# Two 64-byte gaps between the high and low halves of a three-product float32 matmul

## The reference

```
proj = jnp.einsum('bsd,de->bse', h, w_in)                    # 2048 -> 15424
q    = jnp.einsum('bsr,re->bse', _rmsnorm(q_a, ...), w_q_b)  # 512 -> 3072
kv   = jnp.einsum('bsr,re->bse', _rmsnorm(c_kv, ...), w_kv_b)# 512 -> 4096
y_mla, y_conv = ... @ w_o_mla, ... @ w_o_conv                # 2048 -> 2048 each
out  = jnp.einsum('bsd,de->bse', merged, w_out)              # 2048 -> 2048
proj = h @ w_in_2                                            # second block, 272 rows with 16 meta tokens
p    = jnp.einsum('btnc,ncd->btnd', y, w_branch)             # 2 x (1024 -> 2048)
out  = ... @ w_out_2                                         # 2048 -> 2048
```

## Time and profile before

| | |
|---|---|
| median of three runs | 1954.52 us (1952.75 to 1959.03) |
| the profiled execution | 1953.02 us |
| its span, first to last instruction | 1951.6 us |
| PE (matmul) busy | 1937.9 us, 99% of the span, 15818 matmuls |
| PEld (weight load) busy | 1904.6 us, 98% |
| DVE busy | 1175.2 us, 60% |
| ACT busy | 880.6 us, 45% |
| POOL busy | 311.4 us, 16% |
| DMA | 343.80 MB, mean 176 GB/s |

### The profile page before, as it was taken

The page is one execution under the profiler, slowest core; times in us unless marked ns, Lnnn a source line. Parts: engine busy times, 40 slices in busy tenths (PEclk is TensorE's granted clock), DMA queues, the critical chain, the costliest instruction groups (busy, mean ns, idle before and its releaser), DMA issues.

```text
span 1951.6 us, 37152 instructions
## 1 busy us (share of the span) xinstructions
PE 1937.9 (99%) x15818; PEld 1904.6 (98%) x15818; DVE 1175.2 (60%) x1708; ACT 880.6 (45%) x1265; POOL 311.4 (16%) x317
## 2 busy tenths in 40 slices
PE   8999999999999999999999999999999999999999
PEld 8999999999999999999999999999999999999987
DVE  7765666556554545655564665676467776554644
ACT  6444454544444334544445543446443333444443
POOL 3210010202010001300122252040011232110200
PEclk9999999999999999999999999999999999999999
DMA  7565555566666556666565564444565444666564
GB/s 262 154 193 172 165 150 151 172 176 183 193 183 187 188 189 184 181 190 197 189 227 195 176 222 131 141 134 127 160 181 146 131 141 141 174 197 192 184 230 158
DMA packets 175920, 343.80 MB, mean 176 GB/s; under 512 B 10494, under 2 KB 19578, under 8 KB 175226
## 3 DMA queue, kind: packets, MB, share of 16 engines
q1 hardware_dynamic: 174106, 337.16, 56.9%
q10 hardware_dynamic: 1648, 4.26, 0.6%
HBM read 335.09 MB, written 6.29 MB: 175 GB/s over the span
## 4 chain that ended last, share of the span: by engine, by line
PE 94%; DVE 1%; issue 0%; POOL 0%; ACT 0%; POOLq 0%; ACTq 0%; DVEq 0%
PE bank L1289 93%; DVE w_lo L1932 0%; DVE hb L2168 0%; POOL scratch L2528 0%; PE bank L1506 0%; ACT w_hi L1624 0%; PE bank L1444 0%; PE bank L1595 0%; PE bank L1446 0%; PE bank L1445 0%; PE bank L1596 0%; DVE scratch L2038 0%; PE bank L1508 0%; POOL acc_a L2457 0%; POOL arena L2568 0%
## 5 line engine op out<-in xcount | busy, mean ns | idle before, releaser
L1932 DVE TENSOR_TENSOR w_lo<-w_raw,w_hi 128x1024 fp32r<-128x1024 f32 (+2 forms) x644 | 786.5, 1225 | 488.1 <-ACT w_hi L1624 486.7
L1624 ACT ACTIVATE w_hi<-w_raw 128x1024 fp32r<-128x1024 f32 (+2 forms) x644 | 662.9, 1032 | 899.0 <-PE bank L1289 890.0
L1289 PE MATMUL bank<-hb,w_hi 128*128 128x256 f32 x4896 | 868.1, 280 | 1.1 <-DVE hb L1956 0.9
L1289 PEld LDWEIGHTS bank<-hb,w_hi 128*128 128x128 f32 x4896 | 747.5, 188 | 4.1 <-DVE w_lo L1932 2.4
L1289 PE MATMUL bank<-hb,w_lo 128*128 128x256 f32 x2448 | 682.5, 279 | 0.0
L1289 PE MATMUL bank<-ob_hi,w_hi 128*128 128x256 f32 (+1 forms) x2224 | 641.3, 288 | 0.1
L1289 PE MATMUL bank<-ob_hi,w_lo 128*128 128x256 f32 (+1 forms) x2224 | 625.4, 281 | 0.0
L1289 PE MATMUL bank<-ob_lo,w_hi 128*128 128x256 f32 (+1 forms) x2224 | 625.0, 281 | 0.0
L1289 PEld LDWEIGHTS bank<-hb,w_lo 128*128 128x128 f32 x2448 | 460.0, 188 | 0.0
L1289 PEld LDWEIGHTS bank<-ob_hi,w_hi 128*128 128x128 f32 x2224 | 418.3, 188 | 2.5 <-DVE w_lo L1932 0.5
L1289 PEld LDWEIGHTS bank<-ob_lo,w_hi 128*128 128x128 f32 x2224 | 418.4, 188 | 1.6
(11 more groups left out here) (241 smaller groups left out, 1169.5 us busy)
## 6 DMA issues: line engine op xcount, KB each, us to landing
w_raw<-in_w_in SPq DMA_DIRECT2D x436, 512.0 KB, 3.7
w_raw<-in_w_out SPq DMA_DIRECT2D x64, 512.0 KB, 4.2
w_raw<-in_w_o_conv SPq DMA_DIRECT2D x32, 512.0 KB, 3.9
w_raw<-in_w_o_mla SPq DMA_DIRECT2D x32, 512.0 KB, 4.1
w_raw<-in_w_branch SPq DMA_DIRECT2D x32, 512.0 KB, 3.7
w_raw<-in_w_kv_b SPq DMA_DIRECT2D x16, 512.0 KB, 3.8
w_raw<-in_w_q_b SPq DMA_DIRECT2D x16, 384.0 KB, 3.3
arena<-x_kept SPq DMA_DIRECT2D x2, 2048.0 KB, 9.4
```

The costliest lines, as they stand in the source:

```text
L1289: return nc.tensor.matmul(dst, lhsT, rhs, start=start, stop=stop, skip_group_check=True)
L1624: act(dst, src, ACT.Copy).then_inc(S_("w_hi"), 1)
L1932: tt(low, src, high.bitcast(F32), ALU.subtract).then_inc(S_("w_lo"), 1)
```

## The change

Two dummy tensors of 16 floats (64 bytes) are put in, one between `w_hi` and `w_lo`, one between `ob_hi` and `ob_lo`; in `hb` the 64 bytes that lay ahead of both halves now lie between them, and the 64 bytes behind them are gone. All instructions, their order, their waits and their shapes stay as they were; only addresses differ.

```diff
         self.whi = sb("w_hi", [P, N_SPLIT, UNIT], F32R)
+        sb("apart", [P, ODD])
         self.wlo = sb("w_lo", [P, N_SPLIT, UNIT], F32R)
-        hb = sb("hb", [P, ODD + 2 * KT * S + ODD], F32R)[:, ODD:ODD + 2 * KT * S].rearrange("p (k n) -> p k n", k=2 * KT)
-        self.hb_hi, self.hb_lo = hb[:, 0:KT, :], hb[:, KT:2 * KT, :]
-        self.ob_hi, self.ob_lo = (sb(n, [P, KT, T + ODD], F32R)[:, :, 0:T] for n in ("ob_hi", "ob_lo"))
+        hb = sb("hb", [P, KT * S + ODD + KT * S], F32R)
+        self.hb_hi, self.hb_lo = (hb[:, at:at + KT * S].rearrange("p (k n) -> p k n", k=KT) for at in (0, KT * S + ODD))
+        self.ob_hi = sb("ob_hi", [P, KT, T + ODD], F32R)[:, :, 0:T]
+        sb("apart2", [P, ODD])
+        self.ob_lo = sb("ob_lo", [P, KT, T + ODD], F32R)[:, :, 0:T]
```

## The result

The changed kernel takes 1963.46 us (median of seven runs, 1962.88 to 1965.67) against 1956.16 us for the kernel before (seven runs, 1952.75 to 1960.95). The ratio is 1.0043 with a 95% interval from 1.0031 to 1.0055: slower by 0.43%, a small loss, but one that the interval sets apart from no change. The forecast was 1954 us and no change, with 1948 to 1960 us as its own range and 1922 to 1978 us with the rivals.

The account below looks back on a forecast made before the run. PE's distance from one matmul's start to the next was taken as the bound. All terms were 0: span 1951.6 + 0, profiled execution 1953.0, so 1954 us, no change; own range 1948 to 1960 us, 1922 to 1978 us with rivals.

Parts of the forecast that it names:

- the bound: PE, busy 99% of the span: an address change can act only on the distance between matmul starts.
- the cost of the moved tensors to DVE: Subtraction into w_lo, 1224 ns per unit: even a tenth more would go into DVE's idle time; put at 0.
- the two paces: In hb, 256 columns: 117.7 and 113.2 ns on the same addresses, a lock of PE's two streams that a break can switch.
- The sign named for "right": 565 to 640 us again holds 637 to 640 matmuls with 279 to 280 ns records; 1377 to 1396 us again 153.
- each pair of streams that run together keeps its distance exactly: 256-column products: moving operand and the weights loaded beside it keep their address distance modulo 8; 0 us.
- the broken alternation within a kind: 256-column products: the middle matmul starts on the other parity, breaking the alternation twice per triple; taken as 0, range -48 to +29 us.
- rival A: The parity break ends the slow pace: 1927 us for hb alone, 1906 us with ob too; chance 0.24.
- Rival C: Paces redrawn among stretches, 6 us either way, 1948 to 1960 us; beyond the bound 0.06 fast, 0.08 slow.
- Rival B: Equal parities of moving operand and weights clash in two of three pairs: 24 us slower, 1978 us; chance 0.24.
- its aside that the 272-column phases would get a little faster: 272-column stretch: a little faster if equal parities clash, since the same pairing now differs; no size given.
- The rule of the Trainium skill: TensorE has independent read ports for moving operand and weights, and PE never waits on anyone: the change gives 0.
- the 109.2 ns: The skill's back-to-back distance for a 256-column matmul, 256 / 2.4 + 2.5; no stretch of the trace reached it.

Follow-up runs that it names:

- the bare streams: Separate programs with none of the kernel's work: PE alone runs matmul triples at chosen operand placements behind short idle times; 256 columns paced from 113.3 to 120.0 ns.
- 3,4 with 2,3: The change's hb placement: starts of x_hi, x_lo with w_hi, w_lo in 64-byte units modulo 8; run alone on PE, 117.8 ns after all four idle times.
- 5,6 with 2,3: Placement with x_hi, x_lo starting at 5,6 and w_hi, w_lo at 2,3 (64-byte units modulo 8), run alone on PE: 118.5 ns in four of four.
- experiment 7: Kernel before with its tensors reordered and one gap, so hb's x minus w starts are 3 modulo 4 units: 1932.48 us, ratio 0.9878.
- the second trace of before: The kernel before, unchanged, traced once more: 1958.29 us, hb mean 117.42 ns instead of 116.80.
- the halves: Against the kernel before, only w_lo moved by 64 bytes: 1962.97 us; only x_lo, with arena and what lies behind it: 1967.32 us.
- experiment 4: Kernel before with only arena, con, scratch and all behind them moved by 64 bytes, products' operands in place: 1961.38 us, ratio 1.0018.
- 5,5 with 2,2: Placement with x_hi, x_lo both starting at 5 and w_hi, w_lo at 2 (64-byte units modulo 8), alone on PE: 113.3 ns, in some segments 117.8.

## Why the prediction was wrong

Right were the bound (PE's start-to-start distance and nothing else), that no other engine nor DMA sets the pace, that the cost of the moved tensors to DVE is nil (the subtraction into w_lo takes 1225 ns by either page), and that the steps to look at are the products. Right was also that the two paces are states of the same program: the bare streams show both on one placement without any other engine. The sign named for "right", 637 to 640 matmuls in 565 to 640 us, came out too (639), but it couldn't tell anything: that stretch was slow before the change already.

The step that failed is "each pair of streams that run together keeps its distance exactly. Cost: 0 us, if the pace hangs on that pair". The condition doesn't hold. With all distances kept, 3,4 with 2,3 and 5,6 with 2,3 were never fast in 16 segments each, hb in the changed kernel paces at 117.76 ns without a fast stretch, and the version of experiment 7 went from 1932.48 to 1968.88 us when the gaps were put in. Distance matters (6 of 51 against 40 of 52), but only among placements in which all x start at one parity and all w at one. I had seen the other side, the broken alternation within a kind, and given it a price from -48 to +29 us, but no mechanism of its own except as a gain (rival A). It was the reverse: with the break, no placement tried was ever fast (0 of 56 segments).

Rival C had the right place and nearly the right size, and the wrong kind. It said that both fast stretches would be drawn anew and priced their loss at 6 us; hb's mean rose by 0.96 ns, 7226 x 0.96 = 6.9 us (the 6 us had left out the fast matmuls of cin0, nearly 200). But it isn't an even draw: by the bare streams the fast pace is gone, so the loss comes in every run. Against the second trace of before, which had drawn badly, hb lost only 0.34 ns, or 2.5 us. The median of before's seven times, 1956.16 us, lies between the times of the two traces (1953.02 and 1958.29), so the typical loss in hb should lie between as well. To this come 3.0 us in ob, for which I had no term: with alternating blocks the placement of before paces at 117.06 to 117.10 and the changed one at 117.81.

Rival B read the higher pace of 272 columns as the price of equal parity. The bare streams give 126.6 to 126.7 ns at even and uneven starts alike, so its rows didn't bear on it. Its sign was right, and so was its aside that the 272-column phases would get a little faster, but its mechanism was false: the halves would have had to be faster than the whole.

The rule of the Trainium skill that stands beside the forecast (SBUF — State Buffer, "Who interferes with whom": two independent read ports, and PE never waits on anyone) doesn't give these paces: with no other engine at work PE's two streams pace at 113.3, 117.8, 118.5, 119.3 or 120.0 ns by where their operands start. Nor did placement bring any stream down to the 109.2 ns that the prediction set beside its rows; the best is 113.3.

Open is the mechanism underneath: why no placement with mixed parity within a kind is fast, why distance 3 or 7 is fast more often than 1 or 5, and why w_lo may move by two units and x_lo may not. The runs show that these hold for the placements tried, not what arbitrates. How much of the changed kernel's loss comes by the side matmuls' new addresses (experiment 4, 0.18% on its own) is open too.

## What to carry to other kernels

When matmuls of equal form run at two distances from start to start in one trace, look at where their operands start before anything else: keep all moving tiles at one parity of 64 bytes and all stationary tiles at the other, and try the distances 1, 3, 5 and 7 between them, since here the order of a few tensors and one gap were worth about 1.1 to 1.2% (ratios 0.9895 and 0.9878) with no instruction changed. A pairwise argument about what runs beside what isn't enough; a bare program of the inner loop, run behind several slightly different idle times, shows which placements have the fast pace, and roughly how often they find it. And a kernel with such a state has a spread of its own: compare many runs, and don't read one trace's fast stretch as a property of its phase.

## What the hardware showed that I had not expected

- Two stable paces for the same instructions on the same addresses, 113.3 and 117.8 ns for 256 columns at the full clock. In the bare streams one placement had the slow one behind a memset of 9 columns and the fast one behind 10 and 11.
- Equal parity of moving and stationary starts gives 120.0 ns at distance 0 and 118.6 at distance 2 for 256 columns; with 512 columns it was the faster one, 226.7 ns against 228.9 at 3,3 and 233.3 at 5,5 with 2,2; with 272 columns distance 3 paces at 123.3 and distance 1 at 126.7.
- From 5,5 with 2,2 (11 of 20 fast), w_lo moved by 128 bytes is always fast (16 of 16), w_lo moved by 64 bytes never (0 of 4), and x_lo moved by 128 bytes never (0 of 4).
- Moving only tensors that no product reads changed the time by 0.18% (0.08 to 0.29); why is open.
